# Two more seven-product quads per layer in the down projection, with the largest weight sum of each quad made in HBM by an accumulating DMA

## The reference, cut to what matters

```python
def conv_ffn(h, w_up, conv_w, conv_b, w_down):
    u = h @ w_up                       # 2048 -> 8192
    up = jnp.pad(u, ((0, 0), (CONV_W - 1, 0), (0, 0)))
    c = conv_b.astype(h.dtype)
    for tap in range(CONV_W):
        c = c + up[:, tap:tap + S] * conv_w[tap]
    gate, val = jnp.split(c, 2, axis=-1)
    return (jax.nn.gelu(gate, approximate=True) * val) @ w_down

for i in range(DEPTH):                 # DEPTH = 2
    ...                                # hybrid mixer, memory attention
    h = rmsnorm(x, g[4])
    x = x + rmsnorm(conv_ffn(h, w_up[i], conv_w[i], conv_b[i], w_down[i]), g[5])
```

## Time and profile before

| | |
|---|---|
| median of 3 runs | 1966.85 us (1966.82 to 1966.96) |
| profiled execution, its own time | 1967.23 us |
| its span in the profile | 1965.4 us |
| TensorE clock granted, mean | 0.999 |
| busy: PE, weight loads, DVE, ACT, POOL | 99%, 85%, 77%, 58%, 10% |
| down projection of layer 0 | about 820 to 983 us of the span |
| DMA | 394 MB, mean 200 GB/s |

### The profile page before, as it was taken

One profiled execution on the slowest core, in us unless ns is written; L12 is line 12 of the kernel. 1 busy time (PEld: TensorE's weight loads), 2 busy tenths in 40 slices (PEclk: granted clock), 3 DMA queues, 4 the chain that ended last, 5 costly groups with the idle time before them and its releaser, 6 DMA issues.

```text
span 1965.4 us, 30737 instructions
## 1 busy us (share of the span) xinstructions
PE 1952.6 (99%) x10655; PEld 1680.0 (85%) x10655; DVE 1506.6 (77%) x2326; ACT 1138.2 (58%) x1770; POOL 187.2 (10%) x212
## 2 busy tenths in 40 slices
PE   9999999999999999999999999999999999999998
PEld 8888888888888888888888888888888888888886
DVE  7857777857777777788876577768587777778888
ACT  7655566657555555555566655556565555554654
POOL 0010000001222222200000000000012222222000
PEclk9999999999999999999999999999999999999999
DMA  8674558544656666576656444665446666565773
GB/s 319 200 204 155 170 211 241 198 152 169 202 192 207 198 206 200 203 274 240 220 150 229 153 155 160 213 218 196 155 153 205 203 201 209 188 205 210 267 251 135
DMA packets 111490, 393.94 MB, mean 200 GB/s; under 512 B 13140, under 2 KB 14560, under 8 KB 110048
## 3 DMA queue, kind: packets, MB, share of 16 engines
q1 hardware_dynamic: 105632, 368.36, 56.3%
q10 hardware_dynamic: 4448, 20.58, 2.7%
q0 software_dynamic: 1312, 3.70, 0.8%
HBM read 382.35 MB, written 10.24 MB: 200 GB/s over the span
## 4 chain that ended last, share of the span: by engine, by line
PE 98%; DVE 1%; issue 0%; ACT 0%; DMA 0%; DVEq 0%; SPq 0%; ACTq 0%
PE ps L971 24%; PE ps L974 12%; PE ps L881 12%; PE ps L883 11%; PE ps L882 11%; PE ps L893 11%; PE ps L896 5%; PE ps L1298 2%; PE ps L1297 2%; PE ps L1299 2%; PE ps L845 1%; PE ps L1248 1%; PE ps L1236 0%; PE ps L1234 0%; PE ps L1272 0%; PE ps L1260 0%
## 5 line engine op out<-in xcount | busy, mean ns | idle before, releaser
L1778 DVE TENSOR_TENSOR w_lo<-raw,w_hi 128x1024 fp32r<-128x1024 f32 (+2 forms) x660 | 778.6, 1187 | 323.0 <-ACT w_hi L1354 316.9
L1354 ACT ACTIVATE w_hi<-raw 128x1024 fp32r<-128x1024 f32 (+2 forms) x660 | 672.0, 1028 | 345.2 <-PE ps L974 219.7
L971 PE MATMUL ps<-h_t,w_hi 128*128 128x512 f32 x2032 | 639.0, 396 | 0.1
L974 PEld LDWEIGHTS ps<-h_t,w_lo 128*128 128x128 f32 x2032 | 382.1, 188 | 89.7
L974 PE MATMUL ps<-h_t,w_lo 128*128 128x256 f32 x2032 | 399.2, 278 | 0.0
L971 PEld LDWEIGHTS ps<-h_t,w_hi 128*128 128x128 f32 x2032 | 309.3, 189 | 0.3 <-DVE h_t L1796 0.3
L893 PE MATMUL ps<-h_t,w_hi 128*128 128x512 f32 x768 | 246.8, 403 | 0.0
L896 PEld LDWEIGHTS ps<-h_t,w_lo 128*128 128x128 f32 x768 | 144.3, 188 | 33.8
L2522 POOL TENSOR_SCALAR up_c<-up_u,cw 128x256 f32<-128x256 f32 x128 | 130.1, 1027 | 369.6 <-DVE up_u L2356 369.6
L896 PE MATMUL ps<-h_t,w_lo 128*128 128x256 f32 x768 | 151.2, 278 | 0.0
L883 PE MATMUL ps<-w_hi,act_t 128*128 128x512 f32 x320 | 124.5, 389 | 0.0
(11 more groups left out here) (372 smaller groups left out, 2838.4 us busy)
## 6 DMA issues: line engine op xcount, KB each, us to landing
raw<-stream SPq DMA_DIRECT2D x640, 512.0 KB, 4.3
comb<-comb_hbm SPq DMA_DIRECT2D x24, 512.0 KB, 4.8
comb_hbm<-comb_out ACTq DMA_DIRECT2D x14, 512.0 KB, 6.1
raw<-stream SPq DMA_DIRECT2D x24, 288.0 KB, 3.4
raw<-stream SPq DMA_DIRECT2D x16, 262.0 KB, 6.0
gain_a<-gains_in ACTq DMA_DIRECT2D x4, 1024.0 KB, 6.5
m_x<-mem_t_in ACTq DMA_DIRECT2D x2, 2048.0 KB, 11.6
x<-x_in SPq DMA_DIRECT2D x4, 512.0 KB, 13.4
```

The source lines that it names most:

```text
L971: pe.matmul(ps[:, 4 * half + nt, :], hi[:, cc, nt * P:(nt + 1) * P], h_t[:, c, :, :], start=(c == 0), stop=False, skip_group_check=True)
L974: mm = pe.matmul(ps[:, 4 * half + nt, SEQ:2 * SEQ], lo[:, cc, nt * P:(nt + 1) * P], h_t[:, c, 0, :], start=False, stop=(c == KC - 1), skip ...
L1354: act.activation(w_hi[:, slot, 0:width], raw[:, rslot, 0:width], ACT.Copy).then_inc(hi_ready, 1)
L1778: dve.tensor_tensor(w_lo[:, slot, 0:width], raw[:, rslot, 0:width], w_hi[:, slot, 0:width].bitcast(F32), ALU.subtract).then_inc(lo_ready, 1)
```

## The change

`SEVEN` gets a seventh row pair, j = 12, in both passes, so a layer has 14 quads and not 12. `PASS_MID` is reordered: row pairs 2 and 4, and 6 and 8, now stand next to each other in each pass, so that two quads follow each other with no N split between. The sum B is no longer made by DVE: in the attention stage POOL issues, for each quad, a DMA that copies the raw blocks into the HBM tensor `b_hbm` and, when that has landed, a second that adds the other blocks to it. In the down projection ACT loads each B sum (512 KB) from there into one of two tiles `psum_b` (n modulo 2), on ACT's queue. DVE makes the C sums of both quads of a pair ahead of the first. The first half of a D piece is not loaded any more.

```diff
-SEVEN = [0, 2, 4, 6, 8, 10]
-PASS_HEAD, PASS_TAIL = [1, 3], [[14, 15], [12, 14, 15]]
-PASS_MID = [[5, 0, 7, 2, 9, 4, 11, 6, 13, 8, 12, 10], [0, 5, 2, 7, 4, 9, 6, 11, 8, 13, 10]]
+SEVEN = [0, 2, 4, 6, 8, 10, 12]
+PASS_HEAD, PASS_TAIL = [1, 3], [[14, 15], [13, 14, 15]]
+PASS_MID = [[5, 0, 7, 2, 4, 9, 6, 8, 11, 10, 13, 12], [0, 5, 2, 4, 7, 6, 8, 9, 10, 11, 12]]
+SUMS_FROM = 38
...
-                    sp.dma_start(raw[:, p % RAW, :], stream[l * NPIECES + p]).then_inc(landed[p % RAW], 16)
+                    c = 512 if P_DOWN + DOWN_FREED[p - P_DOWN] - 1 in SEVEN_AT else 0
+                    sp.dma_start(raw[:, p % RAW, c:], stream[l * NPIECES + p][:, c:]).then_inc(landed[p % RAW], 16)
...
+                def load_sums(n):
+
+                    m = l * len(SEVEN_AT) + n
+                    if n < 2:
+                        act.wait_ge(*pieces_used(l, P_DOWN - 4 * (1 - n)))
+                        act.wait_ge(b_made, 16 * (l + 1) * len(SEVEN_AT))
+                    else:
+                        act.wait_ge(lo_ready, l * NSPLITS + SEVEN_AT[n - 2] + 4)
+                    if DOWN_SPLITS[SEVEN_AT[n] - P_DOWN][1] == 1 and n % 2 == 0:
+                        act.wait_ge(odd_merged, 2 * l + 1)
+                        act.wait_ge(even_merged, 2 * l + 1)
+                    act.dma_start(psum_b[n % 2][:, 0:2, :], b_hbm[m]).then_inc(b_got[n % 2], 16)
+
+                load_sums(0)
                 for s in range(P_DOWN + SPL, NSPLITS + (2 if l < DEPTH - 1 else 0)):
                     up_tail(UPG // 2 - 1, 1, tail_at(s))
                     split_down(s)
+                    if s == P_DOWN + SPL:
+                        load_sums(1)
+                    for n in range(2, len(SEVEN_AT)):
+                        merged = DOWN_SPLITS[SEVEN_AT[n] - P_DOWN][1] == 1 and n % 2 == 0
+                        if s == max(SEVEN_AT[n - 2] + 5, down_end(1) + SPL + 1 if merged else 0):
+                            load_sums(n)
                     if s == P_DOWN + 20:
...
-                    dve.tensor_tensor(psum_b[:, 0:2, :], raw[:, ra % RAW:rb % RAW + 1, 0:512],
-                                      raw[:, rb % RAW, :].rearrange("p (a n) -> p a n", n=512), ALU.add).then_inc(b_sums, 1)
...
+                    if n > 1:
+                        dve.wait_ge(lo_ready, l * NSPLITS + SEVEN_AT[n - 2] + 4)
+                    dve.wait_ge(*first_sums(l, n))
+                    dve.wait_ge(*raw_landed(l, rb))
+                    dve.tensor_tensor(sums[:, 2, :], sums[:, 0, :], raw[:, rb % RAW, 512:1024], ALU.add).then_inc(b_sums, 1)
+                    dve.wait_ge(b_sums, m + 1)
                     dve.wait_ge(*raw_landed(l, ra))
+                    dve.tensor_tensor(sums[:, 3, :], sums[:, 2, :], raw[:, ra % RAW, 512:1024], ALU.add).then_inc(b_sums, 1)
...
-                    if s + 2 in SEVEN_AT:
-                        first_sums(s + 2)
-                    if s + 1 in SEVEN_AT:
+                    if s + 1 in SEVEN_AT and s - 3 not in SEVEN_AT:
                         other_sums(s + 1)
+                        if s + 5 in SEVEN_AT:
+                            other_sums(s + 5)
...
+                for n, s in enumerate(SEVEN_AT):
+                    p = l * NPIECES + P_DOWN + DOWN_SPLITS[s - P_DOWN][4]
+                    m = l * len(SEVEN_AT) + n
+                    pool.wait_ge(*pieces_used(l, SUMS_FROM + 4 * n))
+                    dst = b_hbm[m].rearrange("p a n -> a p n")
+                    pool.dma_start(dst, stream[p:p + 2, :, 0:512]).then_inc(b_put, 16)
+                    pool.wait_ge(b_put, 16 * (m + 1))
+                    pool.dma_start(dst, stream[p + 1].rearrange("p (a n) -> a p n", n=512), accum_op=ALU.add).then_inc(b_made, 16)
```

More of the change, by code:

```diff
@@ L490, in build @@
         comb = sb("comb", [P, 2, 4, 2, P], 80 * K, F32R)
-        psum_b = sb("psum_b", [P, 4, 512], 88 * K)
+        psum_b = [sb(f"psum_b{i}", [P, 4, 512], at) for i, at in enumerate((88 * K, 104 * K))]
         m1_s = sb("m1_s", [P, 512], 189 * K)
@@ L662, in build @@
         b_sums = sem("b_sums")
+        b_put = sem("b_put")
+        b_made = sem("b_made")
+        b_got = [sem(f"b_got{i}") for i in range(2)]
         m1_copied = sem("m1_copied")
@@ L758, in build @@
         bias_hbm0 = nc.dram_tensor("bias_hbm0", (4 * H_A, 4, 8 * P), F32, kind="Internal").ap()
+        b_hbm = nc.dram_tensor("b_hbm", (DEPTH * len(SEVEN_AT), P, 2, 512), F32, kind="Internal").ap()
         comb_hbm = nc.dram_tensor("comb_hbm", (DEPTH * COMBS, P, 4 * 2 * P), F32, kind="Internal").ap()
@@ L1417, in split_down @@
                         n = l * len(SEVEN_AT) + seven(s - 2 if kind == "B" else s - 3)
-                        act.wait_ge(b_sums, 3 * n + (1 if kind == "B" else 3))
+                        if kind == "B":
+                            act.wait_ge(*first_sums(l, n - l * len(SEVEN_AT)))
+                        else:
+                            act.wait_ge(b_sums, 2 * n + 2)
                         act.wait_ge(split_free, l * NSPLITS + s + 1)
                         c = 0 if kind == "B" else 2
-                        act.activation(w_hi[:, s % SPL, :], psum_b[:, c:c + 2, :].rearrange("p a n -> p (a n)"),
+                        act.activation(w_hi[:, s % SPL, :], psum_b[n % 2][:, c:c + 2, :].rearrange("p a n -> p (a n)"),
                                        ACT.Copy).then_inc(hi_ready, 1)
@@ L1922, in split_down, with other_sums @@
                         c = 0 if kind == "B" else 2
+                        n = seven(s - 2 if kind == "B" else s - 3)
                         dve.wait_ge(hi_ready, l * NSPLITS + s + 1)
-                        dve.tensor_tensor(w_lo[:, s % SPL, :], psum_b[:, c:c + 2, :].rearrange("p a n -> p (a n)"),
+                        dve.tensor_tensor(w_lo[:, s % SPL, :], psum_b[n % 2][:, c:c + 2, :].rearrange("p a n -> p (a n)"),
                                           w_hi[:, s % SPL, :].bitcast(F32), ALU.subtract).then_inc(lo_ready, 1)
-                def first_sums(s):
+                def other_sums(s):
@@ L1941, in other_sums @@
[L1941 to L1948, removed]
+                    m = 2 * (l * len(SEVEN_AT) + n)
@@ new lines, in other_sums @@
+                    sums = psum_b[n % 2]
+                    if n > 1:
[4 more added lines that the diff above has]
+                    dve.wait_ge(b_sums, m + 1)
+                    dve.wait_ge(*raw_landed(l, ra))
+                    dve.tensor_tensor(sums[:, 3, :], sums[:, 2, :], raw[:, ra % RAW, 512:1024], ALU.add).then_inc(b_sums, 1)
@@ L1950, in merge_sums @@
                 def merge_sums(q):
-                    w5, w7, x57 = [psum_b[:, c, :] for c in range(3)]
+                    w5, w7, x57 = [psum_b[0][:, c, :] for c in range(3)]
                     dve.wait_ge(*pieces_used(l, LAST_SEVEN[q] + 1))
@@ L1964, in merge_odd @@
                         dve.wait_ge(*pieces_used(l, GROUP_END[g]))
[L1965 to L1966 removed]
+                    dve.tensor_tensor(acc(l, g, 0), acc(l, g, 0), psum_b[0][:, 0, :], ALU.add)
+                    st.done(dve.tensor_tensor(acc(l, g, 1), acc(l, g, 1), psum_b[0][:, 2, :], ALU.add))
                     dve.sem_inc(odd_merged, 1)
@@ L1973, in merge_even @@
                     dve.tensor_tensor(acc(l, g, 0), acc(l, g, 0), m1_s[:], ALU.add)
-                    st.done(dve.tensor_tensor(acc(l, g, 1), acc(l, g, 1), psum_b[:, 1, :], ALU.subtract))
+                    st.done(dve.tensor_tensor(acc(l, g, 1), acc(l, g, 1), psum_b[0][:, 1, :], ALU.subtract))
                     dve.sem_inc(even_merged, 1)
```

10 lines of the change are left out of this document (4 added, 6 removed).

## The result

The changed kernel takes 2449.27 us (median of 6 runs, 2443.15 to 2453.87) against 1966.95 before (6 runs): a ratio of 1.2449, 95% interval 1.2436 to 1.2462. The forecast was 1973, with a range to 1978. The profiled execution has a span of 2452.1 us, 486.7 more than before.

A forecast was written before the change was run, and what follows sets the result against it. TensorE was taken as the bound, busy 1952.6 of 1965.4 us. From the median of 1966.85 us, 2.7 came off for matmuls saved, and 8.8 and 0.4 were added for late loads: 1973.3, stated as 1973, range 1965 to 1978.

The forecast's parts named there:

- What bounds the kernel, and the gain: TensorE sets the time in the down projection; four more quads save three matmuls each, 2.72 us in all.
- The pair behind gain_f: Down projection, pass 0, second pair: the sum's load queues behind gain_f on ACT, TensorE idles 4.4 us a layer, 8.8 us.
- Ordinary pairs: Down projection, the six other pairs: sum loads landing late idle TensorE 0.4 us together, bounds 0 and six times 1.0.
- The rest: Attention stage: POOL's 28 copies and 28 accumulating DMAs, 12.2 to 18.8 us a quad, were taken to cost nothing.
- a budget of 13.3: Attention stage: the 13.3 us each quad has for its two transfers, as SP moves four pieces at 3.3 us each.
- 26 us of room: Layer 0: how late POOL's sums could end before rm_t, used at 365.4, would be late.
- Rival (c): Attention stage: slow HBM transfers make rm_t some 50 us late in layer 0, above 2000 us; chance 0.02 with other harm.
- POOL's waits stand before nothing due: Attention stage: claimed that POOL's waiting in its queue for the sums' transfers delays nothing due; no cost taken.
- What would show it: The prediction's list of trace signs, such as two TensorE waits of 3 to 5 us, for telling forecast and rivals apart.

The follow-up runs named there:

- e6: e1 with gain_f's load ten splits later and DVE's adds for a pair's second quad behind the first quad's multiplications; 1964.02 us, ratio 0.9985.
- e1: The changed kernel with both HBM-to-HBM transfers of a quad, copy and add, written with 128 rows outermost instead of 2; 1980.51 us, ratio 1.0070.
- e4: e1 with the block that loads gain_f moved ten splits on, from behind split 20 to behind split 30; 1968.78 us, ratio 1.0008.
- e5: e1 with DVE's adds for the second quad of a pair moved behind the low parts of the first, gain_f left in place; 1966.91 us, ratio 0.9999.
- e7: The changed kernel, its slow transfers kept, with rm_t's factor row issued by POOL ahead of the seventh sum instead of behind the fourteenth; 2298.31 us.

## Why the prediction was wrong

**What bounds the kernel, and the gain: right.** Twelve matmuls fewer, and e6 gives the 2.7 us, within its interval.

**The pair behind gain_f: right in place, half right in cause. 8.8 us foreseen, 12.2 measured in the changed kernel** (5.5 and 6.7), 9.4 in e1. The queue held the load: e4, which moves only `gain_f`, cuts these two waits from 9.4 to 3.9 us. But 3.9 us stay without `gain_f` ahead of the load, because it takes 7.3 us there and not the 4.8 that I gave to an undisturbed one. That the landing came out near is partly luck. I had the sum's load issued 2.7 us behind `gain_f` and landing at 12; it is issued 0.9 us behind (at 2.6), takes 10.6 us and lands at 13.2, counted from the first quad's start at 1100.04. The clock that such a wait costs afterwards, 2.2 to 3.0 us each, was not in the sum.

**Ordinary pairs: 0.4 foreseen, 1.4 measured** in the changed kernel, 0.9 in e1. They depend on where DVE's adds stand: in e5, which moves only these, they are gone.

**The step that failed is "The rest"**, with "I take nothing" for the 28 copies and 28 accumulating DMAs. Its bounds, 12.2 to 18.8 us a quad, were taken from `f_k` and the 1 KB store. The first has 128 partitions outermost, the second moves 1 KB, and neither says anything of 512 KB on two engines. The measured price is 25.7 us alone and 37 to 62 beside the stream, against a budget of 13.3. `rm_t` came 281 us late in layer 0 where I had 26 us of room, and TensorE waited 465 us for it in the two layers. Spread (e1), the mean step of 10.4 us is under my lower bound: the bracket was near for the form that I had in mind, not for the form in the diff. What would have given it away stood in the diff: a size of 2 stands outermost in `"p a n -> a p n"`, and no transfer of the trace that I took a price from has that shape. The section of the Trainium skill cited above states the rule, and I didn't put it to this line.

**Rival (c)** named the right chain, slow sums, then `rm_t`, then the attention stage, at 0.02. Its size was 50 us in layer 0 alone, with 18.8 us a quad; it missed that layer 1 has the same queue (213 of the 465 us), and that a sum costs still more beside the stream. The multiplier of 14 was in its sum (14 x 5.5); the price under it was too low. With each microsecond above the budget counted 14 times a layer, the price should have been checked at twice its upper bound.

**"POOL's waits stand before nothing due"** held for the start of the queue only. Behind the fourteenth sum stand `rm_t` and then the pooled adds of `x`; e7 shows both.

**"What would show it"** had the right sign: "POOL's `rm_t` later than 330 us, means (c)". It was 614.95.

## What to carry to other kernels

Before a DMA is priced by another one's duration, compare the shape of the access, above all the size of the outermost dimension: here 512 KB landed after a median of 7.8 us with 128 outermost and 24.5 us with 2, and the two lines that changed this were worth 469 us. Work put on an idle engine's queue is free only as long as the whole series ends before the next item of that queue is due; multiply the upper bound of one by the count, and ask who stands behind the last. Before a wait is put down to one cause, take that cause away alone and look at the same place again: without `gain_f` half of the wait was still there (e4). And where a kernel sits at 99% of TensorE, a wait can cost the clock afterwards too: those of 4.4 us and more did, that of 2.2 us did not.

## What the runs showed of the hardware

- A transfer with outermost dimension 2 inside HBM moves at 53 GB/s as a copy and 26 GB/s as an accumulation, on 0.13 to 0.14 of the engines; spread, they reach 302 and 209 in a slice of 1 us.
- It also makes many small packets: 89812 under 512 B in the changed kernel, 14548 with both transfers spread, 13140 before. Their cause is not shown.
- A transfer behind a slow one on POOL's queue ends, for who waits on it, with the slow one, though by the engines' shares (0.27 for both, 0.14 for the slow one) it is on others and its data moved 10 us before (changed kernel, 577 against 587). POOL waited 25.1 us for `r_hbm<-rst_m`, 1 KB, behind the last add, and 8.9 us in the kernel before, where nothing was ahead of it.
- A load of sums, 512 KB, took 10.6 us 0.9 us behind the 1024 KB of `gain_f` on ACT's queue, and 7.3 us in the same place without it.
- TensorE's granted clock fell to 0.50 after waits of 4.4 us and more and not after 2.2 us; behind a wait it cost 2.2 to 3.0 us.
- ACT issued the load of sums at 1102.65, ahead of the table load (1102.74) and the split (1104.15) that stand before it in the program's order.
